# Which matrices of the last experts stand outside the ring: three down matrices, or two gate/up halves and one down matrix

## What is computed

```python
def run_block(args):
    xblk, e = args
    return (silu(xblk @ w_gate[e]) * (xblk @ w_up[e])) @ w_down[e]
# w_gate, w_up: (2 layers, 32 experts, 1024, 512); w_down: (2, 32, 512, 1024), float32
yb = lax.map(run_block, (xb, blk_e))            # blocks sorted by expert
out = segment_sum(yb * buf_w, buf_tok)          # each token adds its two experts
```

## Time and profile before

| | |
|---|---|
| median of 3 runs | 1744.83 us (1744.66 to 1747.56) |
| the profiled execution | 1747.63 us, of which the span of instructions 1744.6 us |
| mean granted TensorE clock | 0.929 of full |
| busy: PE, DVE, ACT, POOL | 1451.0, 487.4, 459.2, 354.7 us |
| transfers | 473.30 MB, mean 271 GB/s |
| expert stage of layer 0, of layer 1 (first to last product of the experts) | about 488 to 959 us, 1239 to 1716 us |

### The profile page before, as it was taken

The page is one execution under the profiler, slowest core; times in us unless marked ns, Lnnn a source line. Parts: engine busy times, 40 slices in busy tenths (PEclk is TensorE's granted clock), DMA queues, the critical chain, the costliest instruction groups (busy, mean ns, idle before and its releaser), DMA issues. The chain is left out here.

```text
span 1744.6 us, 38984 instructions
## 1 busy us (share of the span) xinstructions
PE 1451.0 (83%) x16162; PEld 936.5 (54%) x16163; DVE 487.4 (28%) x1196; ACT 459.2 (26%) x805; POOL 354.7 (20%) x293
## 2 busy tenths in 40 slices
PE   4999999999787789777689399888878888789883
PEld 4868678686543445443345387556434444345442
DVE  3122112221421112111112669842411211112114
ACT  4232422423312122221122332153112222112222
POOL 2424344342001011000001255521001001001100
PEclk8999999999879999999899699988899898989997
DMA  8212222121489999999999321113599999999985
GB/s 290 97 68 95 80 92 101 50 97 49 168 352 428 428 428 427 429 427 429 427 425 355 137 97 49 51 49 145 219 429 416 403 430 423 428 427 427 412 363 205
DMA packets 65161, 473.30 MB, mean 271 GB/s; under 512 B 6509, under 2 KB 23101, under 8 KB 39506
## 3 DMA queue, kind: packets, MB, share of 16 engines
q1 hardware_dynamic: 60064, 463.56, 64.8%
q0 software_dynamic: 4608, 8.41, 1.3%
q10 hardware_dynamic: 434, 0.51, 0.1%
HBM read 461.96 MB, written 14.68 MB: 273 GB/s over the span
## 5 line engine op out<-in xcount | busy, mean ns | idle before, releaser
L778 PE MATMUL ps<-ring,hgT 128*32 128x256 f32 x6016 | 386.1, 409 | 143.2 <-DMA ring<-w_gu 118.3
L778 PEld LDWEIGHTS ps<-ring,hgT 128*32 128x32 f32 x6016 | 202.9, 116 | 313.4 <-DMA ring<-w_gu 143.3
L434 POOL TENSOR_TENSOR w_lo<-ring,w_hi 128x512 fp32r<-128x512 f32 x176 | 233.8, 1330 | 382.8 <-ACT w_hi L514 382.8
L453 POOL DMA_INDIRECT y_dram<-area_c,idx_s x96 | 94.3, 982 | 790.2 <-ACT area_c L550 771.1
L721 PE MATMUL ps<-area_a,block_rows 128*32 128x256 f32 x3136 | 205.3, 406 | 8.9 <-DVE block_rows L983 8.9
L514 ACT CAST w_hi<-ring 128x512 fp32r<-128x512 f32 x176 | 109.0, 624 | 367.4 <-PE ps L683 367.4
L1105 DVE TENSOR_TENSOR a_e<-sg_e,ps 128x128 f32<-128x128 f32 x94 | 27.0, 287 | 610.3 <-ACT sg_e L545 610.3
L794 PE MATMUL ps<-ring,aT_e 128*32 128x256 f32 x2752 | 166.3, 382 | 23.7 <-DMA ring<-w_down 10.8
L721 PEld LDWEIGHTS ps<-area_a,block_rows 128*32 128x32 f32 x3136 | 112.1, 118 | 87.6 <-issue 32.4
L681 PE MATMUL ps<-w_hi,hT_hi 128*128 128x512 f32 x320 | 126.6, 396 | 7.2 <-DVE hT_lo L1278 7.2
L794 PEld LDWEIGHTS ps<-ring,aT_e 128*32 128x32 f32 x2752 | 83.2, 109 | 85.9 <-issue 22.0
(11 more groups left out here) (192 smaller groups left out, 1514.5 us busy)
## 6 DMA issues: line engine op xcount, KB each, us to landing
ring<-w_gu SPq DMA_DIRECT2D x128, 2048.0 KB
ring<-w_down SPq DMA_DIRECT2D x58, 2048.0 KB
ring<-w_in SPq DMA_DIRECT2D x8, 2048.0 KB
ring<-w_in SPq DMA_DIRECT2D x8, 1024.0 KB
ring<-w_out SPq DMA_DIRECT2D x4, 2048.0 KB
ring<-w_pw SPq DMA_DIRECT2D x8, 1024.0 KB
hT<-w_down SPq DMA_DIRECT2D x2, 2048.0 KB, 7.8
area_c<-w_down SPq DMA_DIRECT2D x2, 2048.0 KB, 8.4
```

The costliest lines, as they stand in the source:

```text
L434: nc.gpsimd.tensor_tensor(w_lo[:, place, :], ring[:, s, at:at + 512], w_hi[:, place, :].bitcast(F32), ALU.subtract).then_inc(lo_ready, 1)
L453: pool.indirect_dma_start(y_dram[l], bass.IndirectOffsetOnAxis(ap=idx_s[:, b:b + 1].bitcast(U32), axis=0), y_out[:, b, :], None, bounds_ch ...
L778: last = nc.tensor.matmul(ps[32 * g:32 * g + 32, 2, 0:256], hgT[:, n * (KT // 2) + k, :], gate_up[n][:, k, :, g * P:(g + 1) * P], start=(n ...
```

## The change

`SPARE` becomes `EARLY`, a list of pairs (expert, part) with part 0 and 1 for the gate/up halves and 2 for the down matrix: `hT` holds gu0 of expert 31, `area_c` gu1 of expert 31, `area_b` the down matrix of expert 30. The down matrices of 29 and of 31 are loaded into the ring. The loops at run time cover experts 2 to 29 in place of 2 to 27 on SP, and 0 to 29 in place of 0 to 27 on PE; 30 and 31 stay written out. The number of loads, their sizes and the waits ahead of each kind are what they were.

```diff
-SPARE = (NE - 3, NE - 2, NE - 1)
+EARLY = ((NE - 1, 0), (NE - 1, 1), (NE - 2, 2))
+LOOPED = (NE - 2) // 2
...
-            early = sum(slots_of[e % 2][2] == s for e in SPARE)
+            early = sum(slots_of[e % 2][part] == s for e, part in EARLY)
...
-                    sp.dma_start(spare[n], w_down[l, SPARE[n]]) \
+                    sp.dma_start(spare[n], (w_gu0, w_gu1, w_down)[EARLY[n][1]][l, EARLY[n][0]]) \
                         .then_inc(spare_loaded[l][n], 16)
...
-                with sp.Fori(1, SPARE[0] // 2) as pair:
+                with sp.Fori(1, LOOPED) as pair:
...
-                for e in range(SPARE[0] // 2 * 2, NE):
-                    s_gu0, s_gu1, s_down = slots_of[e % 2]
+                for e in range(2 * LOOPED, NE):
                     upto = sp.value_load(cum[0:1, e - 1:e], min_val=1, max_val=NBLK - 1)
-                    sp.wait_ge(gu_half[l], upto)
-                    load_expert(s_gu0, w_gu0[l, e])
-                    sp.wait_ge(gu_mm[l], upto)
-                    load_expert(s_gu1, w_gu1[l, e])
-                    if e not in SPARE:
-                        sp.wait_ge(y_mm[l], upto)
-                        load_expert(s_down, w_down[l, e])
+                    for part, (left, w) in enumerate(((gu_half, w_gu0), (gu_mm, w_gu1), (y_mm, w_down))):
+                        if (e, part) not in EARLY:
+                            sp.wait_ge(left[l], upto)
+                            load_expert(slots_of[e % 2][part], w[l, e])
...
+            def one_block(l, t, pair, slots, e=None):
+
+                def weights(part):
+
+                    at = EARLY.index((e, part)) if (e, part) in EARLY else None
+                    return ring[:, slots[part], :] if at is None else spare[at]
+
+                def loaded(part):
+
+                    if (e, part) in EARLY:
+                        pe.wait_ge(spare_loaded[l][EARLY.index((e, part))], 16)
+                    else:
+                        s = slots[part]
+                        pe.wait_ge(slot_loaded[s], 16 * pair + (expert_base(l, s) + 16))
...
-                for e in range(SPARE[0] // 2 * 2, NE):
+                for e in range(2 * LOOPED, NE):
                     first = pe.value_load(cum[0:1, e:e + 1], min_val=0, max_val=NBLK - 2)
                     after = pe.value_load(cum[0:1, e + 1:e + 2], min_val=1, max_val=NBLK - 1)
                     with pe.Fori(first, after) as t:
-                        one_block(l, t, e // 2, *slots_of[e % 2], early=SPARE.index(e) if e in SPARE else None)
+                        one_block(l, t, e // 2, slots_of[e % 2], e)
```

## The result

| | before | after |
|---|---|---|
| median of 20 runs | 1744.88 us (1739.63 to 1747.56) | 1749.18 us (1747.09 to 1755.14) |
| ratio to before | | 1.0034 (95%: 1.0024 to 1.0043) |
| the profiled execution, its span | 1747.63, 1744.6 us | 1750.03, 1748.0 us |
| mean granted TensorE clock | 0.929 | 0.934 |

A forecast was written before the change was run, and what follows sets the result against it. PE, not the weights' stream, was taken to bound the end of each expert stage. 1747.63 + 3.3 (wait) + 1.7 (clock) + 0.1 (loop) = 1752.7, less 2.8 to the median: 1749.9 us, range 1746.8 to 1752.6.

The forecast's parts named there:

- the loop: Experts 28 and 29 run in a loop instead of written-out code: entering expert 29 costs 0.50 us for 0.39, sum +0.1.
- What bounds the end: End of the expert stage: PE sets it, not the stream, which has run dry by 937 in layer 0.
- The order of the stream and who is late: Loads behind gu1 of expert 28: down 29 now comes ahead, so both halves of expert 30 come one load later.
- The size of the wait: Layer 0, second half of expert 30: lands at 932.2, wanted at 928.95, PE 3.3 us later; bounds 3.1 to 4.3.
- The clock: Behind the new wait in layer 0, PE loses clock: 1.7 us, about two in three; bounds 0 and 1.7.
- case 2: Layer 0, expert 30: the wait without a loss of clock, 1748.2 us, own range 1747.4 to 1749.0; chance 0.27.
- case 1: The forecast: layer 0, second half of expert 30 late, one clock loss beside it; 1749.9 us, 1749.0 to 1751.0; chance 0.43.
- Rival 3: Layer 0: median runs lack the clock loss at 902.66; new wait 5.0 us, clock loss behind; 1751.6 us; chance 0.14.
- Subtracting 2.8 us to come from the profiled execution to the median: Whole kernel: the profiled execution, 1747.63, lies 2.8 us over the median of 1744.83, cause unnamed, so 2.8 is taken off.
- The sum 1752.7: Whole kernel, against the profiled execution: 1747.63 + 3.3 + 1.7 + 0.1 us, before 2.8 is taken off.
- Layer 1: Last experts of layer 1: the stream has room, so no wait and no gain; only the loop's +0.1 us.
- The rule on branches: Looped experts: taken branches can miss prefetched code, so written-out code is preferred; by rows worth 0.1 us.

## Why the prediction was right, step by step

The time, the sign and the place were right; 1749.9 was forecast and 1749.18 measured, inside the range. That it is as near as 0.7 us is partly luck: the wait and the loop came out 0.8 us larger together, the loss of clock, counted whole, is there in some profiles and not in others, and 2.8 us were taken off for a reason that wasn't known.

- **What bounds the end.** Right, PE in both layers. Its test is the kernel with all of 31 outside the ring, which gained nothing, against those that take away the waits at or ahead of 28, which did.
- **The order of the stream and who is late.** Right, and shown from both sides: with down 29 outside the ring the wait is gone, with the change in layer 0 alone the whole loss is there.
- **The size of the wait.** The term that was too small. Six loads were to take 29.58 us, as between the second halves of 26 and 28; between those of 28 and 30 the trace of the changed kernel has 933.14 - 903.07 = 30.07, and the other kernels with this wait 30.43, 30.06 and 929.18 - 898.94 = 30.24 with 28 to 31 written out. So 3.3 became 3.84, inside the bounds of 3.1 to 4.3. It isn't that the changed kernel's stream was slower: between 26 and 28 it took 29.57. The later stretch is the slower one (see the last section). The prediction put the difference between its estimate of 4.81 us for a load and 4.93 down to the scatters; from 873.08 to 902.66 their queue took 1.3% of the engines' time, and 4.93 is 2.5% over 4.81, so that they account for about half. The first half of 30 was said to be 0.3 us late; its idle grew from 0.52 to 1.37, by 0.85.
- **The clock.** Counted as two in three. Behind the new wait the changed kernel's profile has full clock; the other three kernels with this wait lost it. So the profiled execution is case 2 of the rivals, those of the other three are like case 1. Whether that changes between executions of one kernel isn't shown, as each kernel has one profile. Both are here, first the changed kernel, then the one with 28 to 31 written out (third number from the end):

```profile
933.00:935.00 2.00, 1.86 (x36) 1.18 (x40) 0.00 (x0) 0.00 (x0) 0.00 (x0) 1.00 0.92 391
935.00:938.00 3.00, 2.86 (x51) 1.53 (x47) 0.98 (x4) 0.54 (x2) 0.00 (x0) 1.00 0.36 153
...
929.00:931.80 2.80, 2.62 (x32) 1.42 (x36) 0.00 (x0) 0.00 (x0) 0.00 (x0) 0.67 0.88 375
931.80:935.50 3.70, 3.56 (x47) 1.84 (x43) 0.75 (x4) 0.54 (x2) 0.00 (x0) 0.79 0.14 58
```

  In the second, 0.33 x 2.8 + 0.21 x 3.7 = 1.7 us were lost, the size that was said. The traces' terms without it make 3.84 + 0.36 = 4.2 us, with it 5.9; the medians differ by 4.3, the ratio gives 5.9 (4.2 to 7.5). The times can't say how often it falls; both are within.
- **Rival 3.** It took it that without the loss of clock at 902.66 PE would reach expert 30 1.7 us earlier, and so wait 5.0 there. The kernel with the change in layer 1 alone, whose layer 0 has the places of before, has no such loss in its profile:

```profile
901.50 1.93 PE L788 MATMUL ps<-ring,hgT 128*32 128x256 f32 x32 [2.87 <-DMA ring<-w_gu]
...
907.26 1.93 PE L801 MATMUL ps<-ring,aT_e 128*32 128x256 f32 x32 [1.63 <-DMA ring<-w_down]
```

  PE only waits for the down matrix of 28 in its place: 5.76 us from one line to the other, before 908.62 - 902.66 = 5.96. So by this profile that loss costs 0.2 us and not 1.7, and a wait of 5.0 wouldn't arise. Behind the new wait the down matrix of 30 stands outside the ring and hides nothing: 937.41 - 933.14 = 4.27 us with full clock, 937.22 - 931.26 = 5.96 with the loss, in the kernel with layer 0 alone.
- **Subtracting 2.8 us to come from the profiled execution to the median.** Some 1.0 of these 2.8 us lies outside the instructions: that execution took 3.03 us more than its span, 33 other executions of the same kernel 1.8 to 2.4, and the changed kernel's 2.03. What the rest is was not found. The 20 runs of the kernel before range over 8 us, so one profile stands anywhere in that. The sum 1752.7 for a profiled execution was 2.7 over the 1750.03 of the one that was taken: 1.7 of it is the clock, 1.0 the time outside the span. The rest nearly cancels: the wait and the loop took 0.8 more, and layer 1 took 0.9 less from SP's first load of the stage to the second half of 28 (409.84 us, before 410.78).
- **Layer 1.** No wait, as said. The loop's term was too small: 0.36 in place of 0.1. The trace has its parts: expert 29 entered with 0.49 in place of 0.38, expert 30 with 0.61 in place of 0.51, and 31, for a reason not found, with 0.37 in place of 0.52; and blocks of 28 and 29, now in the loop, wait 0.21 for ACT ahead of the down product, where written-out ones don't, 0.08 a block over four blocks. Why a block in the loop has this wait in layer 1 is open.
- **The rule on branches** (the Trainium skill, Runtime: NRT & Kernel Launch, Instruction fetch mechanics). It pointed the right way (the loop is dearer), at a price that the times can't show: the kernel with the written-out code has 1.0027, the change 1.0034, with intervals that overlap. No run shows that the fetching of instructions is what costs here.

## What to carry to other kernels

When a stream of loads in a fixed order bounds a stage, a buffer outside the stream is worth something only for a matrix at which the consumer waits or ahead of it; at the last consumers, if these are bound by their own work, it gains nothing, and each load that it puts ahead of a matrix which comes just in time costs its own time less the slack (here 4.93 us less some 1.6, so 3.3 expected and 3.84 measured). So read the consumer in order of time, mark the last wait that a transfer ends, and number the loads behind it before and after. And when a buffer is freed from the ring, relax the waits of the loads that used to follow it, and look for the hole that this leaves: here, in layer 0, that was worth 3.3 us by the traces.

## What was not expected of the hardware

The pace of the same full stream isn't fixed. From the second half of expert 26 to that of 28, six loads of 2 MB took 29.57 to 30.04 us in seven profiles (29.58 before, 29.57 after). The next six, to the second half of 30, took 30.06 to 30.43 in the four profiles where PE waited for them, and in each of these four more than the six ahead of them, by 0.16 to 0.74 us. All transfers together ran at 424 to 429 GB/s in every one of these stretches. What differs is the queue of the scatters: it moved 0.14 to 0.23 MB in the first stretch and 0.30 to 0.39 MB in the second, though three scatters were issued in each. In the four kernels the difference is 0.09 to 0.24 MB, which at some 425 GB/s is 0.2 to 0.6 us, an estimate that is near the time lost. No run changed the scatters, so this cause is argued and not shown.
